# Expert panels of a mixture-of-experts stage in another order: down panels ahead of the next expert's last gate panel, and the second pair's wide products in two halves on other banks

## The reference, cut to what matters

```python
def expert_block(args):
    xblk, e = args
    a = xblk @ w_gate[e]
    b = xblk @ w_up[e]
    return (jax.nn.silu(a) * b) @ w_down[e]

yb = lax.map(expert_block, (xb, block_expert)).reshape(P, D)
out = jnp.zeros((N + 1, D), jnp.float32).at[slot_tok].add(yb.astype(jnp.float32) * slot_gate[:, None])
```

## Time and profile before

| | us |
|---|---|
| device time, median of 3 runs | 1925.93 |
| device time of the profiled execution | 1925.25 |
| its span | 1923.3 |
| PE busy | 1823.6 (95%) |
| DVE busy | 938.7 (49%) |
| ACT busy | 591.4 (31%) |
| POOL busy | 79.5 (4%) |
| HBM read | 322.45 MB |

### The profile page before, as it was taken

The page is one execution under the profiler, slowest core; times in us unless marked ns, Lnnn a source line. Parts: engine busy times, 40 slices in busy tenths (PEclk is TensorE's granted clock), DMA queues, the critical chain, the costliest instruction groups (busy, mean ns, idle before and its releaser), DMA issues.

```text
span 1923.3 us, 24206 instructions
## 1 busy us (share of the span) xinstructions
PE 1823.6 (95%) x9862; PEld 1307.7 (68%) x9862; DVE 938.7 (49%) x1571; ACT 591.4 (31%) x1056; POOL 79.5 (4%) x89
## 2 busy tenths in 40 slices
PE   7999999999988999999998999999988999999996
PEld 7878888888867787777777767789773333333332
DVE  4344555455465564445457565654672333333233
ACT  5443233232333323323336443423331111110102
POOL 0000000000000000000000000061011000000000
PEclk8999999999999999999999999999999999999999
DMA  6412222122212122222122132200378999999996
GB/s 248 173 66 88 77 88 99 66 98 90 97 57 98 66 84 82 77 77 99 66 77 77 44 110 88 88 1 12 131 313 316 421 420 420 420 421 420 421 420 255
DMA packets 50752, 325.65 MB, mean 169 GB/s; under 512 B 8088, under 2 KB 8264, under 8 KB 14032
## 3 DMA queue, kind: packets, MB, share of 16 engines
q1 hardware_dynamic: 44464, 305.65, 40.7%
q0 software_dynamic: 6032, 17.39, 2.6%
q10 hardware_dynamic: 144, 1.05, 0.1%
HBM read 322.45 MB, written 5.31 MB: 170 GB/s over the span
## 4 chain that ended last, share of the span: by engine, by line
PE 74%; DMA 9%; DVE 8%; ACT 4%; issue 3%; SPq 1%; another core or an unknown queue 1%; POOL 0%; DVEq 0%; ACTq 0%; POOLq 0%
PE PJ L564 15%; PE PJ L566 15%; PE PJ L565 15%; PE PJ L2438 8%; PE PJ L2452 4%; DMA m_d<-in_w_moe 3%; DMA m_a<-in_w_moe 3%; DMA m_b<-in_w_moe 3%; PE PB L2464 2%; PE PB L2153 2%; PE PB L2114 1%; PE PB L2233 1%; PE PB L2146 1%; PE PB L2247 1%; DVE x L1439 1%
## 5 line engine op out<-in xcount | busy, mean ns | idle before, releaser
L564 PE MATMUL PJ<-hT_hi,w_hi 128*128 128x512 f32 x832 | 338.7, 407 | 7.5 <-DVE x L1439 6.1
L1237 DVE TENSOR_TENSOR w_lo<-w_raw,w_hi 128x1024 fp32r<-128x1024 f32 (+1 forms) x224 | 228.3, 1032 | 206.6 <-ACT w_hi L794 205.8
L566 PE MATMUL PJ<-hT_hi,w_lo 128*128 128x512 f32 x832 | 325.4, 391 | 0.0
L565 PE MATMUL PJ<-hT_lo,w_hi 128*128 128x512 f32 x832 | 324.7, 390 | 0.0
L794 ACT ACTIVATE w_hi<-w_raw 128x1024 fp32r<-128x1024 f32 (+1 forms) x224 | 196.1, 899 | 37.3 <-PE PJ L566 25.3
L564 PEld LDWEIGHTS PJ<-hT_hi,w_hi 128*128 128x128 f32 x832 | 156.7, 188 | 54.7 <-issue 20.7
L566 PEld LDWEIGHTS PJ<-hT_hi,w_lo 128*128 128x128 f32 x832 | 156.4, 188 | 34.2
L565 PEld LDWEIGHTS PJ<-hT_lo,w_hi 128*128 128x128 f32 x832 | 157.0, 189 | 33.4 <-issue 3.4
L848 ACT ACTIVATE sc<-sc,stats 128x256 f32<-128x256 f32 (+2 forms) x80 | 43.4, 542 | 330.9 <-DVE stats L1320 330.9
L2438 PE MATMUL PJ<-m_b,xT 128*64 128x512 f32 x496 | 117.6, 601 | 7.0 <-DMA m_b<-in_w_moe 6.9
L1864 DVE TENSOR_TENSOR x<-x,PB 128x512 f32<-128x512 f32 x128 | 79.5, 682 | 84.5 <-PE PB L2464 84.4
(11 more groups left out here) (425 smaller groups left out, 2889.5 us busy)
## 6 DMA issues: line engine op xcount, KB each, us to landing
w_raw<-in_w_all SPq DMA_DIRECT2D x92, 1024.0 KB, 4.8
m_b<-in_w_moe SPq DMA_DIRECT2D x86, 1024.0 KB, 26.9
m_a<-in_w_moe SPq DMA_DIRECT2D x66, 1024.0 KB, 26.4
m_c<-in_w_moe SPq DMA_DIRECT2D x20, 1024.0 KB, 27.3
m_d<-in_w_moe SPq DMA_DIRECT2D x10, 1024.0 KB
m_e<-in_w_moe SPq DMA_DIRECT2D x10, 1024.0 KB
aux<-scr_c POOLq DMA_DIRECT2D x6, 512.0 KB, 4.0
aux<-in_decay POOLq DMA_DIRECT2D x6, 512.0 KB, 4.3
```

What stands on the lines that cost most here:

```text
L564: pe.matmul(dst, lh, rh, start=start, stop=False)
L565: pe.matmul(dst, lh, rl, start=False, stop=False)
L566: return pe.matmul(dst, ll, rh, start=False, stop=stop)
L1237: dve.tensor_tensor(w_lo[:, n % SPLIT, j * w:(j + 1) * w], w_raw[:, n % RAW, j * w:(j + 1) * w], w_hi[:, n % SPLIT, j * w:(j + 1) * w].bit ...
```

## The change

The change has four parts.

1. `panel_order` puts the two down panels of expert e - 1 between gate panels 2 and 3 of expert e. For the last expert, 31, it is gate 0 to 2, down 4 of expert 30, gate 3, down 5 of expert 30. Loads and uses follow the same list.
2. The loop of TensorE follows it. The transpose of the next pair's rows now stands behind gate panel 3 (for pair 1 between the two down panels of expert 0). The hidden values of expert 31 are transposed behind both down panels of expert 30, not between them.
3. `second_rows` is split. Its first four products go to PB2, right behind gate panel 3 of expert 0, and no longer wait on `r_hc`. Its other four go to PB3, in turn 1 behind the transpose of expert 0's hidden values. `r_hc` is waited on before the transpose of pair 1's rows.
4. ACT and DVE follow. ACT copies y of expert e - 1 out before the tanh of expert e (in turn 31: after it). DVE has the copies of pair 1 and `table_out` at the head of turn 1, ahead of the hidden values of expert 1, and makes `yl` at the head of each turn. GpSimd reads the table back before it waits for the wide products, and not after.

```diff
     for e in range(NE + 1):
-        if e < NE:
-            order += [(e, j) for j in range(4)]
-        if e:
-            order += [(e - 1, j) for j in (4, 5)]
+        gate = [(e, j) for j in range(4)] if e < NE else []
+        down = [(e - 1, j) for j in (4, 5)] if e else []
+        if e == NE - 1:
+            order += gate[0:3] + down[0:1] + gate[3:] + down[1:]
+        else:
+            order += gate[0:3] + down + gate[3:]
...
-            pool.wait_ge(r_x1, 1)
+            pool.wait_ge(r_sc, 128)
+            for par in range(2):
+                pool.dma_start(ix[par * CAP:par * CAP + CAP, :, :],
+                               A["scr_tab"].rearrange("(p b) o -> p b o", p=CAP)).then_inc(r_ix, 16)
+            pool.wait_ge(r_x1, 2)
...
+                if e == 1:
+                    dve.wait_ge(r_x1, 2)
+                    dve.tensor_copy(xs[:, 1, S:2 * S], PB[3][:]).then_inc(r_xc, 1)
+                    dve.wait_ge(x_tr, 2)
+                    x_copy_dve(1).then_inc(x_cd, 1)
+                    table_out()
+                if 0 < e < NE - 1:
+                    dve.wait_ge(y_ev, e)
+                    y_low((e - 1) % 2)
...
+            def second_rows(c):
+                if c == 0:
+                    pe.wait_ge(r_oh, 4 * NT)
+                for t in range(NT):
+                    last = pe.matmul(PB[2 + c][:], OH[:, t, P:2 * P], xn_t(6, t)[:, c * S:(c + 1) * S],
+                                     start=(t == 0), stop=(t == NT - 1))
                 last.then_inc(r_x1, 1)
...
+            for e in range(NE):
+                if e % 2 == 0:
+                    pe.wait_ge(x_ca, e // 2 + 1)
+                    pe.wait_ge(x_cd, e // 2 + 1)
+                if e >= 2:
+                    pe.wait_ge(h_mid, e - 1)
+                for j in range(3):
+                    if j == 2 and e:
+                        hidden_turn(e - 1)
+                    if j == 2 and e == 1:
+                        second_rows(1)
+                    gate_up(e, j)
                     if e % 2 and e >= 3 and j % 2 == 0:
                         pair_combine((e - 3) // 2, j)
                         pair_combine((e - 3) // 2, j + 1)
+                if e:
+                    down(e - 1, 0)
+                if e == 1:
+                    transpose_next(1)
+                if e == NE - 1:
+                    gate_up(e, 3)
+                if e:
+                    down(e - 1, 1)
+                if e < NE - 1:
+                    gate_up(e, 3)
                 if e == 0:
-                    second_rows()
+                    second_rows(0)
+                elif e > 1 and next_pair(e):
+                    transpose_next(next_pair(e))
...
+            hidden_turn(NE - 1)
+            for j in range(2):
+                down(NE - 1, j)
```

98 lines of the change are left out of this document (37 added, 61 removed).

## The result

| | before | after |
|---|---|---|
| median, us | 1925.47 (6 runs, 1923.53 to 1926.22) | 1915.59 (6 runs, 1913.86 to 1917.17) |
| ratio | | 0.9950, 95% interval 0.9937 to 0.9962 |
| profiled execution | 1925.25 | 1914.69 |
| its span | 1923.3 | 1912.8 |
| first gate panel to gate panel 0 of expert 31 | 447.95 | 439.32 |

The forecast was 1917.3 in a range from 1915.9 to 1921.0. The kernel is faster, as forecast, but the median lies 1.7 us under the forecast and 0.3 under the range. The interval of the ratio is 7.3 to 12.1 us of gain, so the 8.6 us that were forecast lie inside it: the miss itself is not clear of the noise of six runs.

The account below looks back on a forecast made before the run. Weight transfers bound the end, with a hole of 8.5 us near 1454 to 1464. Profiled 1925.25 - 8.2 (hole) - 0.4 (last expert) = 1916.6, plus 0.7 to the median: 1917.3, range 1915.9 to 1921.0.

Parts of the forecast that it names:

- Where the time is lost: From 1454 to 1464 us few weights move because wide products free no slots; 8.5 us of transfer lost.
- The first wide products: At expert 0, without the wait for DVE, the first half takes 3.53 us at full clock, ending at 1448.9.
- the second half: Behind two gate panels of expert 1 and the hidden-value transpose, it runs to 1456.4; TensorE is then 7.7 us earlier.
- the issues of SP: SP issues the next six panels at 1450.9 to 1464.8, each in time to leave no hole in transfers.
- The hole closes: The 8.5 us stretch without transfers after expert 0 disappears, less 0.3 at hand-overs: -8.2 us.
- Down panels earlier, the table: In every turn mT and row copies stay covered, and the table read in turn 1 causes no wait: 0 us.
- The last expert: From expert 31's gate panel 0 to its last two panels, 16.5 us against 16.9: gains 0.4.
- The profiled execution: Whole kernel under the profiler: 1925.25 - 8.2 - 0.4 = 1916.6 us.
- The median: Median of runs lies 0.7 us above the profiled execution, as before the change, so 1917.3.
- Rival A: TensorE was busy to 1449.1 in expert 0's gate panels, its records wrong; only 5.7 us gained, 1920.2; chance 16%.
- B: Hand-overs between transfers after the first wide products leak 1 us each; at worst 1924.2, no change; chance 7%.
- C: Down panels wait for mT in each of 31 turns, making it slower, 1935.9 at 2.0 us delay; chance 3%.

Follow-up runs that it names:

- e2: Kernel before with only the wide products split in two halves, the first without the r_hc wait, panel order as before: 1916.47 us, ratio 0.9985.
- e15: Kernel before with GpSimd's eight scatters held until behind expert 0's first four gate panels: 1921.57 us, ratio 1.0017.
- e7: Changed kernel with GpSimd's eight scatters held until behind expert 0's first four gate panels, chip b: 1914.51 us, one run.
- e14: Changed kernel with GpSimd's eight scatters held until behind expert 0's first four gate panels, chip d: 1916.26 us, ratio 0.9988 to the kernel before.
- e17: Changed kernel with GpSimd's scatters behind expert 0's first four gate panels, once more, on chip b: 1917.16 us, ratio 0.9997 to the kernel before.
- e8: Changed kernel with expert 31 in the same panel order as all other experts: 1918.57 us, ratio 0.9994 to the kernel before.
- e1: Changed kernel run again without an edit, on chip a: 1916.27 us, ratio 0.9984 to the kernel before.
- e18: Kernel before, unchanged, run again on chip b for its profile: 1917.95 us, ratio 1.0000.
- e6: Kernel before with 20 unused identity-matrix matmuls ahead of the r_hc wait, to keep the clock up: 1921.35 us, ratio 1.0015.
- e10: Kernel before with eight extra tanhs, each waited for, delaying expert 0's own tanh, on chip c: 1928.95 us, ratio 1.0021.
- e9: Kernel before, unchanged, profiled on chip c: 1926.28 us, one run.
- e11: Changed kernel with eight extra tanhs, each waited for, delaying expert 0's own tanh, on chip c: 1918.87 us, ratio 0.9965 to the kernel before.
- e12: Kernel before with eight extra tanhs delaying expert 0's, plus 19 identity-matrix matmuls ahead of the r_hc wait to keep the clock up: 1927.32 us, ratio 1.0015.
- e4: Changed kernel with the r_hc wait put back ahead of the first half of the split wide products: 1916.81 us, ratio 0.9991 to the kernel before.
- e3: Changed kernel with the wide products whole again behind the r_hc wait, keeping the new panel order: 1918.30 us, ratio 0.9999 to the kernel before.

## Why the prediction was right, and where it was wrong

*Where the time is lost.* Right. The loss was a stretch without transfers, its cause the slots that the wide products kept from coming free, and e2 shows that their split alone brings the way down.

*The first wide products, the second half, the issues of SP.* Right to 0.2 us at each of the six issues, and so were the granted clock and the 3.5 us of a half.

*The hole closes, with 0.3 given back at hand-overs: -8.2.* The mechanism is right, and the term was mis-sized by 0.43: it measured -8.63. I had counted only the ten us from 1454 to 1464. A second, small dip of before, 262 GB/s from 1468 to 1470 or 0.75 us, is not in the term, and it went too:

```profile
1468.00:1470.00 2.00, 2.00 (x13) 1.01 (x13) 1.63 (x7) 0.77 (x2) 0.00 (x0) 1.00 0.86 262
```

Three stretches, counted from each kernel's own first gate panel, 0 to 16, 16 to 26 and 26 to 40 us, first of before, then of after, give the whole account:

```profile
1438.32:1454.32 16.00, 11.02 (x43) 4.04 (x40) 2.62 (x8) 0.38 (x1) 7.22 (x8) 0.84 0.86 310
1454.32:1464.32 10.00, 10.00 (x32) 3.64 (x32) 0.69 (x1) 0.73 (x2) 2.11 (x3) 0.92 0.20 59
1464.32:1478.32 14.00, 14.00 (x70) 4.94 (x68) 3.70 (x10) 2.21 (x5) 2.16 (x2) 1.00 0.99 398
```

```profile
1436.97:1452.97 16.00, 16.00 (x68) 5.74 (x65) 2.63 (x8) 1.25 (x3) 7.62 (x9) 1.00 0.86 303
1452.97:1462.97 10.00, 10.00 (x45) 3.68 (x45) 3.58 (x9) 1.20 (x2) 2.82 (x5) 1.00 1.01 407
1462.97:1476.97 14.00, 14.00 (x70) 4.85 (x66) 3.10 (x6) 2.34 (x5) 2.01 (x2) 1.00 1.01 414
```

Against 420 GB/s before falls short by 4.2, 8.6 and 0.7 us, after by 4.5, 0.3 and 0.2. So the hand-overs did give back 0.5 us in the last two stretches, close to the 0.3 of the forecast, and the first stretch another 0.3; what was missing in the term is the 0.75 of the second dip. That dip was there to be read beforehand. The total was not: before alone falls short by 13.5 us over these 40, of which the change could win only 8.6.

*Down panels earlier, the table: 0.* Right. No down panel waited for `mT` before the last expert, and DVE read the table without a wait. Its cover is limited: e15 shows what a table that is 5.9 us later does in the order of before (5.05 us of TensorE), e7, e14 and e17 that in the changed order one that is 5.9 to 6.1 later costs TensorE 2.8 to 2.9.

*The last expert: -0.4.* It measured -0.51. TensorE waits 0.60 us for `mT` and not 0.97, as worked out. e8 shows that without its own order this would have been +0.9, and 1.7 more behind the mark, since the clock falls there.

*The profiled execution: 1916.6.* It measured 1914.69, 1.9 less, and here lies most of the miss: 0.43 is the hole's term, 0.11 the last expert's, and 1.35 a term that the sum put at nothing without a word, the start of the experts. It came 1.35 us sooner than in the profile before. The change does nothing there, and in later profiles of the same two kernels the first gate panel came at 1437.6 and 1442.1 (before) and at 1439.9 and 1440.6 (changed), so this was chance; the rival that code ahead of the experts had become faster, which e1 was to test, would have kept it under 1437.3.

*The median: + 0.7 over the profiled execution.* It measured +0.90, so the step itself held, by luck: it takes the distance of one execution to a median of three for the distance of any. In medians the 1.75 us of the miss are 0.54 from the two terms, 0.46 by which the median before came down when three more runs were added, and 0.75 that are neither way nor tail. A range whose low end, 1915.9, is worked out from terms of the way and the tail alone has no room for that; it should have had the scatter of the runs of before in it, 1.1 us over three runs, beside the terms.

*Rival A, TensorE not idle.* Refuted by the trace after: with the fourth answer again late (1447.73), the next panels were issued at 1449.57 and 1451.29, two gate panels behind wide products that so had begun by 1444. TensorE was free and the semaphore was late. e18 says it from the other side: on another chip the same matmuls are answered at 7.11. *B and C* did not come about; e6 gives the slope of C's kind, 2.7 us for 3.1 of delay.

*What it took as given.* I read the late semaphore as a question about TensorE's records and priced it as a rival. It comes and goes with the chip or the occasion, and it makes most of the gain: the kernel before took 1924.6 to 1925.5 where the answers were late and 1918.4 to 1919.0 where they came at once, and there the same change brings 3 us. That the forecast came within 2 us hung on the comparison falling on the late kind, as the profile before had. Nothing in the one trace could tell that, but the rows showed a lag with no cause, and a forecast should say which of its terms hang on such a row.

## What to carry to other kernels

Where transfers set the end, go through the rate stretch by stretch up to where it is steady. What it falls short of the steady rate is an upper bound (13.5 us here); the gain is the part of it that the change fills (the hole and the dip behind it, 9.4), less what stays or comes anew at hand-overs (0.8). Look for the longest piece of work that frees no slot, and split it or take its wait away; here that, and not the new order of the panels, made the way shorter. A gain that rests on a lag for which the trace shows no cause should be forecast for both cases, with and without it.

## What the runs showed of the hardware

*TensorE's semaphore is seen late on some occasions.* While expert 0's four gate panels run, beside GpSimd's eight scatters, SP's answers came 1.95, 3.67, 5.39 and 7.11 us behind the first of them on three chips, in every profile. On two occasions, the first comparison and chip c, they came at 3.6, 6.5, 7.9 and 10.8 (before, after, e10; within 0.2), or the first only at 7.9 to 9.3 and the other three within 2.3 us behind it (e9, e11, e12). ACT's tanh, which waits for the same matmuls, was as late (1447.82 in the changed kernel):

```profile
1447.82 0.38 ACT L1166 ACTIVATE th<-PJ 128x256 f32<-128x256 f32 x1 [11.10 <-remote]
```

In all six profiles with the delay, that tanh starts 1.5 to 1.9 us behind the end of the last scatter, in the changed kernel behind this one:

```profile
1445.35 0.97 POOL L735 DMA_INDIRECT scr_tab<-tg,di  x1 [0.31 <-issue]
```

The form goes with the scatters too: where the answers began at 3.6 the first of the eight scatters was issued 0.65 us ahead of the first gate panel, where they began at 7.9 or later 2.3 us ahead. That fits scatters that delay the semaphore, but the same scatters delay nothing on the other chips, at either distance (e1 and e4), and the kernels with later scatters (e7, e14, e15, e17) all fell on those. The cause stays open.

*The clock after idle time.* With 1.3 us of idle time ahead of the wide products the granted clock stayed at 1.00, that is 2.4 GHz (e3, e18); with 3.73 or more it went to about 0.5, 1.2 GHz (e9, e10), and the first half took 5.2 to 6.4 us in place of 3.5. In between the length alone did not decide: behind 2.84 us it was at 0.50 in e2 (first row), behind 2.92 us still at 1.00 in e7 (second row), and in e8 it fell behind waits of 1.46 and 0.47 us with a transpose between them.

```profile
1468.00:1470.00 2.00, 1.34 (x4) 0.59 (x6) 1.16 (x2) 0.00 (x0) 1.57 (x2) 0.50 1.02 430
```

```profile
1468.00:1470.00 2.00, 0.64 (x4) 0.40 (x6) 1.26 (x3) 0.17 (x1) 1.52 (x2) 1.00 1.01 422
```

*The start of the stage moves.* Over the twenty profiles the first gate panel came between 1436.38 and 1443.65, over those of the kernel before without an edit between 1437.63 and 1442.13. That is more than the 3 us that the change gains where the answers are prompt, so a difference of one us is read from the way and the tail sooner than from the whole time.
